# Stick-breaking attention and HGRN2: weight loads, output-weight pieces and query/key turns moved to later uses, SP's program written out, and the values' two parts made by GpSimd

## The reference, cut to what matters

```python
u = rms_norm(h, norm_gain)
q, k, v, gate = jnp.split(u @ w_in, 4, axis=-1)
q = rms_norm(split_heads(q), q_gain)
k = rms_norm(split_heads(k), k_gain)
z = (q @ k.T) * scale                       # per head, s < t only
log_skip_j = where(causal, log_sigmoid(-z), 0)
log_skip = reverse_cumsum(log_skip_j) - log_skip_j
weights = where(causal, exp(log_sigmoid(z) + log_skip), 0)
h = h + ((weights @ v) * silu(gate)) @ w_out
```

## Time and profile before

| | |
|---|---|
| median of three runs | 1176.01 us |
| the profiled execution | 1174.98 us |
| its span in the profile | 1173.3 us |
| PE busy | 1145.6 us, 98% of the span |
| PEld, DVE, ACT, POOL busy | 1048.3, 831.4, 419.7, 162.5 us |
| DMA | 141.78 MB, mean 121 GB/s |
| granted clock of TensorE | 1.0 of full speed |

### The profile page before, as it was taken

One profiled execution on the slowest core, in us unless ns is written; L12 is line 12 of the kernel. 1 busy time (PEld: TensorE's weight loads), 2 busy tenths in 40 slices (PEclk: granted clock), 3 DMA queues, 4 the chain that ended last, 5 costly groups with the idle time before them and its releaser, 6 DMA issues. The chain is left out here.

```text
span 1173.3 us, 19984 instructions
## 1 busy us (share of the span) xinstructions
PE 1145.6 (98%) x7012; PEld 1048.3 (89%) x7012; DVE 831.4 (71%) x1636; ACT 419.7 (36%) x887; POOL 162.5 (14%) x344
## 2 busy tenths in 40 slices
PE   8999999898999999999999999999999999999998
PEld 8999989898988989888888989898999999999787
DVE  5768786858687775774444778788888888788421
ACT  5554454444444444452222222323232322222200
POOL 2413131213122231110003100000000000000000
PEclk9999999999999999999999999999999999999999
DMA  8243545455454531066632110314242421107441
GB/s 251 56 120 113 172 145 183 154 149 185 145 173 136 153 99 46 1 237 209 208 108 72 55 37 19 115 67 137 74 141 71 135 84 45 46 37 292 153 139 72
DMA packets 145214, 141.78 MB, mean 121 GB/s; under 512 B 19936, under 2 KB 117472, under 8 KB 145120
## 3 DMA queue, kind: packets, MB, share of 16 engines
q1 hardware_dynamic: 106336, 120.88, 31.5%
q10 hardware_dynamic: 38784, 19.67, 6.2%
HBM read 93.86 MB, written 46.66 MB: 120 GB/s over the span
## 5 line engine op out<-in xcount | busy, mean ns | idle before, releaser
L28 PE MATMUL p_proj<-w_qkv_hi,ut_hi 128*128 128x384 f32 x504 | 171.9, 341 | 0.4 <-DVE ut_lo L911 0.4
L30 PE MATMUL p_proj<-w_qkv_hi,ut_lo 128*128 128x384 f32 x504 | 169.0, 335 | 0.0
L29 PE MATMUL p_proj<-w_qkv_lo,ut_hi 128*128 128x384 f32 x504 | 168.8, 335 | 0.0
L28 PE MATMUL p_proj<-w_ig_hi,next_hi 128*128 128x256 f32 x512 | 145.5, 284 | 0.0
L29 PE MATMUL p_proj<-w_ig_lo,next_hi 128*128 128x256 f32 x512 | 143.1, 279 | 0.0
L30 PE MATMUL p_proj<-w_ig_hi,next_lo 128*128 128x256 f32 x512 | 143.0, 279 | 0.0
L28 PE MATMUL p_proj<-next_hi,w_qf_hi 128*128 128x512 f32 x282 | 113.2, 401 | 0.0
L923 DVE TENSOR_TENSOR_SCAN a_skip<-a_skip,a_diagonal 128x641 f32<-128x641 f32 (+3 forms) x64 | 86.7, 1355 | 35.1 <-ACT a_beta L742 30.5
L30 PE MATMUL p_proj<-next_hi,w_qf_lo 128*128 128x512 f32 x282 | 110.1, 390 | 0.0
L29 PE MATMUL p_proj<-next_lo,w_qf_hi 128*128 128x512 f32 x282 | 109.9, 390 | 0.0
L28 PEld LDWEIGHTS p_proj<-w_ig_hi,next_hi 128*128 128x128 f32 x512 | 96.2, 188 | 0.0
(11 more groups left out here) (258 smaller groups left out, 2790.3 us busy)
## 6 DMA issues: line engine op xcount, KB each, us to landing
stage<-in_hg_w_in_dram SPq DMA_DIRECT2D x32, 512.0 KB, 4.6
stage<-in_sb_w_in_dram ACTq DMA_DIRECT2D x24, 512.0 KB, 5.3
w_out_hi_scratch<-m_in SPq DMA_DIRECT2D x32, 256.0 KB, 2.1
w_out_lo_scratch<-m_in SPq DMA_DIRECT2D x32, 256.0 KB, 2.5
m_in<-mixed_scratch SPq DMA_DIRECT2D x12, 448.0 KB, 6.0
a_gated<-in_x_dram SPq DMA_DIRECT2D x8, 512.0 KB, 3.9
m_in<-in_sb_w_out_dram SPq DMA_DIRECT2D x16, 256.0 KB, 3.4
ut_hi<-w_out_hi_scratch SPq DMA_DIRECT2D x8, 512.0 KB, 8.1
```

Of the source, the lines that this page charges most:

```text
L28: pe.matmul(out, w_hi, m_hi, start=start, stop=False, skip_group_check=True)
L29: pe.matmul(out, w_hi, m_lo, start=False, stop=False, skip_group_check=True)
L30: return pe.matmul(out, w_lo, m_hi, start=False, stop=stop, skip_group_check=True)
```

## The change

- The three loads of query, key and value weights, which ACT issued together at the end of use 9 for head h + 3 (and at the end of step -1 for head 2), are issued one each at the end of uses 4, 5 and 6, for head h + 2. The gate's load stays at use 7; its split goes from use 5 to use 6.
- The pieces of the output weights are loaded after the carry of k = 1 (two pieces), 5 and 6, split at the end of uses 4, 5, 7 and 8, and stored after the carries of k = 4, 5 and 7, the last piece of a group after the first carry of the next head. So head 5 stores one piece too.
- In PLAIN steps PE turns query and key at kt = 5 in place of kt = 2.
- SP's loop over heads 1 to 4 is unrolled.
- Both parts of the values are made by POOL, behind the scaling of the keys of the same tile. The rounded part is a product with a broadcast one.

```diff
+            "one": sb("one", [P, 1]),
...
-    SPLIT_AT = [0, 1, 5, 6]
-    SPLITS_AFTER = {0: ("store", 0), 1: ("store", 1), 3: ("load", 2), 4: ("load", 3), 5: ("store", 2), 6: ("store", 3)}
+    SPLIT_AT = [4, 5, 7, 8]
+    SPLITS_AFTER = {4: [("store", 0)], 5: [("store", 1), ("load", 2)], 6: [("load", 3)], 7: [("store", 2)]}
+    TURN_AT = 5
...
@@ sync: carry no longer waits on w_parts_stored between the two reads of tile 7 of the order @@
-            def carry_all(h, b, group, previous=None):
-
-                if group is not None:
-                    for i in range(2):
-                        load_raw_half(sp, m_in, w_out, link, group, i)
-                for j in range(TILES):
-                    carry(h, j, group if j == TILES - 1 else None)
-                    if j == 0 and previous is not None:
-                        store(previous, 1 - b)
-                    if group is not None and j in SPLITS_AFTER:
-                        ...
+            def carry_all(h, b):
+
+                group = h - 1
+                for k in range(TILES):
+                    carry(h, k)
+                    if k == 0 and h >= 1:
+                        store(h - 1, 1 - b)
+                    if k == 0 and group >= 1:
+                        store_half(sp, m_in, w_out, link, group - 1, 3)
+                    if k == 1 and group >= 0:
+                        if group >= 1:
+                            for i in range(2):
+                                sp.wait_ge(link["w_parts_stored"][i], group * 64)
+                        if group < 4:
+                            for i in range(2):
+                                load_raw_half(sp, m_in, w_out, link, group, i)
+                    if 0 <= group < 4:
+                        for what, part in SPLITS_AFTER.get(k, []):
+                            ...
-            carry_all(0, 0, None)
-            with sp.Fori(0, 2) as pair:
-                for b in (1, 0):
-                    carry_all(pair * 2 + 2 - b, b, pair * 2 + 1 - b, pair * 2 + 1 - b)
-            carry_all(HEADS - 3, 1, None, HEADS - 4)
+            for h in range(CARRIED):
+                carry_all(h, h % 2)
...
@@ scalar, and the same condition in vector @@
-                    if projects and i == (5 if plan is PLAIN else 3):
+                    if projects and i == (6 if plan is PLAIN else 3):
                         split_hi(n, 3)
...
-                    if plan is FIRST and i == USES - 1:
-                        for p in range(3):
-                            load(2, p)
...
-                    if plan is PLAIN and i == 7:
-                        load(h + 2, 3)
-                    if plan is PLAIN and i == USES - 1 and not (isinstance(h, int) and h == HEADS - 3):
-                        for p in range(3):
-                            load(h + 3, p)
+                    if plan is PLAIN and 4 <= i <= 7:
+                        load(h + 2, i - 4)
...
@@ vector @@
-                        if not (isinstance(n, int) and n < 2):
-                            dve.wait_ge(o_done, PAIRS * (n - 1))
...
-                        dve.tensor_copy(v_hi[nb][:, t, :], raw[t % 4][:, 2, :]).then_inc(v_hi_ready, 1)
-                        dve.wait_ge(v_hi_ready, NAT * n + t + 1)
-                        dve.tensor_tensor(v_lo[nb][:, t, :], raw[t % 4][:, 2, :], v_hi[nb][:, t, :].bitcast(F32),
-                                          ALU.subtract).then_inc(v_ready, 1)
...
@@ gpsimd, after the product that scales the keys @@
+            pool.memset(c["one"][:, :], 1.0)
...
+                    if not (isinstance(n, int) and n < 2):
+                        pool.wait_ge(o_done, PAIRS * (n - 1))
+                    pool.tensor_tensor(v_hi[nb][:, i, :], raw[i % 4][:, 2, :], c["one"][:, 0:1].to_broadcast([P, P]),
+                                       ALU.mult).then_inc(v_hi_ready, 1)
+                    pool.wait_ge(v_hi_ready, NAT * n + i + 1)
+                    pool.tensor_tensor(v_lo[nb][:, i, :], raw[i % 4][:, 2, :], v_hi[nb][:, i, :].bitcast(F32),
+                                       ALU.subtract).then_inc(v_ready, 1)
...
@@ tensor @@
-                            if i >= 3 and i % 2 == 1 and kt == (KT - 2 if plan is SQUEEZED and i == 9 else 2):
+                            if i >= 3 and i % 2 == 1 and kt == (KT - 2 if plan is SQUEEZED and i == 9 else
+                                                            TURN_AT if plan is PLAIN else 2):
                                 turn_qk(h, (i - 3) // 2, plan)
```

More of the change, by code:

```diff
@@ L591, in load, with carry @@
                 load_columns(sp, stage, w_in, h, p).then_inc(w_loaded[p], 16)
-            def carry(h, k, group):
+            def carry(h, k):
                 sp.wait_ge(flipped, TILES * h + k + 1)
@@ L599, in carry @@
                 for c in range(2):
-                    if c == 1 and group is not None:
-                        for i in range(2):
-                            sp.wait_ge(link["w_parts_stored"][i], group * 64 + 64)
                     read_flipped(sp, h, k, c)
-            def carry_all(h, b, group, previous=None):
-                if group is not None:
-                    for i in range(2):
-                        load_raw_half(sp, m_in, w_out, link, group, i)
-                for j in range(TILES):
-                    carry(h, j, group if j == TILES - 1 else None)
-                    if j == 0 and previous is not None:
-                        store(previous, 1 - b)
-                    if group is not None and j in SPLITS_AFTER:
-                        what, part = SPLITS_AFTER[j]
-                        if what == "load":
-                            load_raw_half(sp, m_in, w_out, link, group, part)
-                        else:
-                            store_half(sp, m_in, w_out, link, group, part)
+            def carry_all(h, b):
[15 more added lines that the diff above has]
+                        for what, part in SPLITS_AFTER.get(k, []):
+                            if what == "load":
+                                load_raw_half(sp, m_in, w_out, link, group, part)
+                            else:
+                                store_half(sp, m_in, w_out, link, group, part)
             def store(h, b):
```

## The result

The changed kernel takes 1194.97 us (median of 4 runs, 1190.97 to 1202.16) against 1176.55 for the kernel before (4 runs beside it): a ratio of 1.0165, 95% interval 1.0104 to 1.0226. The forecast was 1169.5 with 1179 as its upper end; it was wrong in its sign. The profiled execution took 1198.6 us, its span 1196.9, which is 23.6 above the span before.

The account below looks back on a forecast made before the run. PE was busy 1145.6 of 1173.3 us; latency chains through tiles 5 and 7 set its stops, ceiling 24.0 us. Terms -9.1 + 1.2 + 1.2 + 0.3 = -6.4 gave 1168.6 profiled, 1169.6 median (1169.5 given), range 1160 to 1179.

Parts of the forecast that it names:

- The later loads and SP's waits for splits at k = 4, 5 and 7: Uses 5 to 7: only small tiles are met, no cost in the sum; without cover, third pair stops up to 1 us a head.
- The first load: Behind the copy of use 4: 512 KB beside tile 7's read, 0.2 us in each of six heads, +1.2 us.
- The turn: Query and key turned at kt = 5: 6.3 us of waits go, the second outputs' stop grows as much; 0.
- Values: Values made by POOL: meetings with DVE in the critical legs cost 0.2 us a head, +1.2 us.
- rival C: POOL's values hold DVE at instruction changes in the chain, 1.95 us a head: slower, 1180 us; chance 0.13.
- Step -1: POOL's norms of x stand behind the two new values instructions: +0.3 us, ends 0 and 1.0.
- First leg: First score matmul to landing of tile 5's store: shorter as loads leave use 9 and pieces uses 0 and 1; -9.1 us.
- Second leg 21.0 to 21.5: Landing of tile 5's store to the second pair of outputs: a sign expected after the change; wrong if changed over 1 us.
- If PE stops at a place where it didn't before: Sign of being wrong: PE stops at a new place, such as the third pair or the gate's weights.

Follow-up runs that it names:

- loads alone: Kernel before with only the query, key and value weight loads moved to uses 4 to 6 and the gate's split to use 6: ratio 1.0067.
- the run with one load at use 4: Kernel before with the first of the three loads at the end of use 4 and the other two at the end of use 8: ratio 0.9979, 1174.22 us.
- the turn alone: Kernel before with only the turn of query and key moved to kt = 5: ratio 1.0045.
- loads at uses 5 and 6: Kernel before with the first load at the end of use 8, the second and third at the end of uses 5 and 6: ratio 0.9976, 1175.28 us.

## Why the prediction was wrong, by its own steps

- **"The later loads and SP's waits for splits at k = 4, 5 and 7 meet only the small tiles: the lo part of tile 3 is ready 1.7 us before its outputs."** This step failed, and it is the largest: 14.3 us of stops at the last pair, 1.3 at a third, and 8.5 of the 11.9 us of clock behind three of them. I put these loads at nothing in the sum, and took the cover of one tile for that of three in a row. Where one 512 KB load stands ahead of a store it costs 2.1 us (loads alone, head 0), not the 1.25 that I had from SP's stores. Three stores lost 3.3, 3.8 and 1.9 us in head 1 behind loads; SP and ACT, in order, handed the delay on and added it up. The next head's weight splits stood in the same queues, ahead of the last tile. I had named the third pair and 1 us; it was the last pair and 2.4 to 4.7.
- **The first load, "+1.2", ends 0 and 7.5.** By the run with one load at use 4 it is 0.45% (5.3 us) against use 8: inside the ends, far from the value taken. The mechanism was another: I priced the read of tile 7, which the load left alone, and not the store at k = 4 behind it, which it made 1.9 to 2.9 us longer in five heads.
- **The turn, 0, ends 0 and +1.** The waits behaved as forecast (22.3 for 22.1), the end was wrong: +5.3 us, because two short stops made one long one and the granted clock fell. A stop had no price but its length anywhere in my sum. Filling it made the loss go away.
- **Values, +1.2, ends 0 and 12.** Alone +7.5. The meetings on DVE cost less than forecast (0.1 us a head), so rival C did not come about in its mechanism, although its side of the result did. The exclusive lock of the Trainium skill (SBUF - State Buffer, "SBUF: two separate sides") would cost DVE up to the whole 0.4 us of a product or difference; the most that a multiply lost is 0.16. What the profiles show in its place is second legs 0.4 us longer, stops of 2.0 to 2.5 where 1.6 to 2.0 had stood, and a lower clock behind four of them.
- **Step -1, +0.3, ends 0 and 1.0.** Measured 1.9 by the profile: POOL's norms of x stood on PE's path there. Between the medians with and without it nothing can be told.
- **First leg, -9.1.** The stops at the old places fell from 24.0 to 14.8 (-9.2), but this agreement is luck. From a head's first score matmul to the landing of tile 5's store the kernel after takes 14.4, 16.6, 16.6, 15.8 and 15.7 us in heads 1 to 5, against 16.2, 16.9, 17.8, 19.0 and 15.2 before: 5.9 us less in all, where 14.2 in head 1 and 14.95 in heads 2, 4 and 5 were forecast. The stops shrank by more than the legs because PE, at a lower clock right behind the last pairs' stops of heads 1, 2 and 4, did its work in the next heads more slowly: from the first scores to the second outputs, less the stops, it took some 7 us more in all. The mechanism held where the loads do no harm: in the kernel after with its loads at use 8 the legs are 14.4, 14.8, 14.9, 15.1 and 15.1, as forecast, and in the kernel before with its loads there they are 9.2 us shorter in all, of which 7.8 us reach the time. But the pieces had no part in it (0.9934 without, 0.9942 with).
- **Second leg 21.0 to 21.5.** It held in the kernel after in heads 1, 2 and 5 (21.17, 21.30, 21.10), missed in 3 and 4 (21.94, 21.65), and head 0's 22.73 came in large part from a read of tile 5 of 5.2 us. It takes about 5 us in most kernels here; the profile before (3.78) is one of the few exceptions, so this isn't the change.
- **"If PE stops at a place where it didn't before"** was the sign I gave for being wrong, and it is what happened.

What stays open: why the second leg is longer with the values on GpSimd beyond DVE's 0.1 us a head, what the gate's split at use 6 takes of the loads' loss, why the clock falls behind some stops and not behind longer ones, and why single stores take 5 us with nothing beside them.

## What to carry to other kernels

A transfer that is moved must be priced against every store and read that is under way with it, on whatever queue it is, and its delay followed through each in-order engine to the **last** user, since delays of successive tiles add up. The harmless place for the loads was here where their buffers have just come free and the next latency chain hasn't begun: one use earlier gave 0.66%, three to five uses earlier, with the gate's split one later, took 0.67%. And on TensorE a stop is not priced by its length alone: two stops merged into a longer one can cost more than both.

## What the runs showed of the hardware that was not expected

- After single stops of TensorE of 2.1 to 4.7 us its granted clock was at 0.50 for some microseconds, and 1.7 or 3.4 us of clock were lost each time (2.06 us before the second pair of head 1 in the kernel after with its turn undone, 4.71 in the kernel after). It was not so after each: stops of 3.3 us with the turn alone and of 3.18 in the kernel after were followed by 1.00 throughout, and so were all stops, up to 2.0 us long, in the profile of the kernel before.
- A tile's store at k = 5 that takes 2.0 to 2.2 us without a load takes 4.4 with one 512 KB load issued 1.3 us ahead on the other engine's queue (loads alone, head 0), 2.6 with one issued 3.7 us ahead (loads at uses 5 and 6, head 0), and 5.3 with a load and two stores of 256 KB (kernel after, head 1).
- A 128 x 128 product or difference on GpSimd takes 0.40 to 0.46 us in step -1 and 0.75 and 0.62 us on average in the kernel after. In the kernel before with the values on GpSimd, DVE's scan and multiply of tile 7 became 0.06 and 0.04 us longer on average, single ones by up to 0.11 and 0.16.
